# Copying turned attention probabilities out of PSUM with one engine or with two, one head each

## The reference

```python
# first block, per head
s_own = jnp.einsum('bhqd,bhpd->bhqp', qb, kown).astype(f32) * scale + bias_own
p = jax.nn.softmax(logits, axis=-1)
out = jnp.einsum('bhqp,bhpd->bhqd', p_own, vown)

# second block, per head
p_cmp = _softmax_f32(logits, valid) * valid
o_sel = jnp.einsum("bghtk,bgtkd->bghtd", p_sel, vs)
o_win = jnp.einsum("bghtk,bgkd->bghtd", p_win, vw)
out = gc[..., 0:1] * o_cmp + gc[..., 1:2] * o_sel + gc[..., 2:3] * o_win
```

## Time and profile before

| | us |
|---|---|
| median of 3 runs | 1717.1 (1715.51 to 1721.55) |
| the profiled execution's own time | 1719.34 |
| its span, first to last instruction | 1717.4 |
| TensorE busy in the span | 1679.1 |
| VectorE busy | 938.7 |
| ScalarE busy | 720.3 |

### The profile page before, as it was taken

How to read it: one execution, slowest core, us unless ns; L and a number is a source line. 1 busy time by engine, 2 the same in 40 slices (tenths; PEclk the granted TensorE clock), 3 DMA queues, 4 the chain that set the end, 5 groups by cost and what they waited for, 6 DMA issues and landing times.

```text
span 1717.4 us, 26172 instructions
## 1 busy us (share of the span) xinstructions
PE 1679.1 (98%) x11461; PEld 1530.6 (89%) x11466; DVE 938.7 (55%) x928; ACT 720.3 (42%) x822; POOL 58.9 (3%) x72
## 2 busy tenths in 40 slices
PE   8998999999999999999999999999999999899999
PEld 6987899989889998999989899998999987689998
DVE  5476644455564445554576545455545485754544
ACT  5404443444444344443443434345434334753432
POOL 0023000000000000000000000000000030000000
PEclk9999999999999999999999999999999998999999
DMA  9544546457354644655565564656564534036461
GB/s 294 186 75 124 190 163 216 155 184 231 123 190 167 216 154 171 221 183 185 176 208 167 174 209 157 212 172 201 191 220 150 194 117 160 2 130 213 152 217 74
DMA packets 221649, 297.15 MB, mean 173 GB/s; under 512 B 7403, under 2 KB 184767, under 8 KB 221536
## 3 DMA queue, kind: packets, MB, share of 16 engines
q1 hardware_dynamic: 215256, 284.39, 49.5%
q10 hardware_dynamic: 6280, 11.09, 2.8%
HBM read 291.27 MB, written 3.15 MB: 171 GB/s over the span
## 4 chain that ended last, share of the span: by engine, by line
PE 89%; DVE 5%; ACT 3%; DMA 2%; issue 1%; POOL 0%; SPq 0%; ACTq 0%; DVEq 0%; POOLq 0%
PE ps L1739 20%; PE ps L1639 16%; PE ps L1640 16%; PE ps L1642 16%; PE ps L1661 3%; PE ps L1655 3%; PE ps L1656 3%; DVE wlo L1087 2%; PE ps L1686 2%; PE ps L1687 1%; PE ps L1688 1%; ACT whi L623 1%; DMA raw<-in_hgrn_w_out 1%; PE ps L1677 1%; PE ps L2048 1%
## 5 line engine op out<-in xcount | busy, mean ns | idle before, releaser
L1087 DVE TENSOR_TENSOR wlo<-raw,whi 128x2048 fp32r<-128x2048 f32 (+2 forms) x270 | 602.5, 2251 | 228.7 <-ACT whi L623 228.1
L1639 PE MATMUL ps<-xhi,whi 128*128 128x256 f32 x2432 | 599.6, 284 | 4.8 <-DVE xlo L1113 4.8
L1640 PE MATMUL ps<-xhi,wlo 128*128 128x256 f32 x2432 | 597.7, 283 | 0.0
L623 ACT ACTIVATE whi<-raw 128x2048 fp32r<-128x2048 f32 (+1 forms) x265 | 497.9, 1900 | 114.4 <-DMA raw<-in_hgrn_w_out 40.3
L1639 PEld LDWEIGHTS ps<-xhi,whi 128*128 128x128 f32 x2432 | 467.2, 192 | 7.5 <-issue 5.2
L1640 PEld LDWEIGHTS ps<-xhi,wlo 128*128 128x128 f32 x2432 | 467.6, 192 | 2.3
L1642 PE MATMUL ps<-xlo,whi 128*128 128x256 f32 x2432 | 341.4, 283 | 0.0
L1642 PEld LDWEIGHTS ps<-xlo,whi 128*128 128x128 f32 x2432 | 313.7, 192 | 0.0
L690 ACT ACTIVATE hhi<-hid 128x512 fp32r<-128x512 f32 x54 | 34.1, 632 | 511.0 <-DVE hid L1150 461.1
L1150 DVE TENSOR_TENSOR hid<-silu,ps 128x512 f32<-128x512 f32 x60 | 41.3, 688 | 319.5 <-PE ps L1642 319.5
L1739 PE MATMUL ps<-whi,hhi 128*128 128x512 f32 x480 | 187.5, 391 | 0.0
(11 more groups left out here) (229 smaller groups left out, 1328.4 us busy)
## 6 DMA issues: line engine op xcount, KB each, us to landing
raw<-in_ffn_w_gate_up SPq DMA_DIRECT2D x80, 1024.0 KB, 5.6
raw<-in_ffn_w SPq DMA_DIRECT2D x62, 1024.0 KB, 5.7
raw<-in_ffn_w_down SPq DMA_DIRECT2D x44, 1024.0 KB, 5.6
raw<-in_hgrn_w_in SPq DMA_DIRECT2D x16, 1024.0 KB, 5.7
raw<-in_moba_w_in SPq DMA_DIRECT2D x12, 1024.0 KB, 5.7
raw<-in_conv_w_in SPq DMA_DIRECT2D x10, 1024.0 KB, 5.2
raw<-in_ffn_w_gate_up SPq DMA_DIRECT2D x16, 512.0 KB, 5.3
raw<-in_kv_w SPq DMA_DIRECT2D x6, 1024.0 KB, 5.1
```

Of the source, the lines that this page charges most:

```text
L623: act.activation(whi[s % WRING][:, 0:width], raw[n % RING][:, 0:width], ACT.Copy).then_inc(split_hi, 1)
L1087: ins = dve.tensor_tensor(wlo[s % WRING][:, part], raw[n % RING][:, part], whi[s % WRING][:, part].bitcast(F32), ALU.subtract)
L1639: pe.matmul(out, hi[:, k, tile], xhi[:, k, :], start=k == 0, stop=False)
L1640: pe.matmul(out, lo[:, k, tile], xhi[:, k, :], start=False, stop=False)
```

## The change

The copy of a unit's turned probabilities is divided by head. ScalarE copies the first head's 384 elements from bank 4 and signals `pt_ready` as before. VectorE copies the second head's 384 elements from bank 5 in a new function, `keep_other`, with a new semaphore, `pt_other_ready`. TensorE waits for both where it waited for one. In `attention`, `keep_other(i - 1)` is put on VectorE's queue directly behind `scale_probs(i - 1)`, ahead of `y_low` and of the maxima of the next iteration. In `moba` the copies stand at the head of the next unit's work. The new copy waits for the same two things as ScalarE's: the turn of this unit, and the values of two units before.

```diff
--- before.py
+++ after.py
@@ -381,6 +381,7 @@
         probs_ready = sem("probs_ready")
         probs_turned = sem("probs_turned")
         pt_ready = sem("pt_ready")
+        pt_other_ready = sem("pt_other_ready")
         pv_done = sem("pv_done")
         gate_kept = sem("gate_kept")
         gated = sem("gated")
@@ -821,7 +822,7 @@
                 act.wait_ge(probs_turned, at.att + u + 1)
                 if u >= 2:
                     act.wait_ge(pv_done, at.att + u - 1)
-                act.activation(att_pt[:, u % 2, :, :], ps[:, 4:6, 0:3 * P], ACT.Copy).then_inc(pt_ready, 1)
+                act.activation(att_pt[:, u % 2, 0, :], ps[:, 4, 0:3 * P], ACT.Copy).then_inc(pt_ready, 1)
 
             def y_high(pair, units, dst, src):
 
@@ -1334,6 +1335,13 @@
                         ins = dve.tensor_scalar(x, x, coef[:, b, n:n + 1], None, ALU.mult)
                 ins.then_inc(probs_ready, 1)
 
+            def keep_other(u):
+
+                dve.wait_ge(probs_turned, at.att + u + 1)
+                if u >= 2:
+                    dve.wait_ge(pv_done, at.att + u - 1)
+                dve.tensor_copy(att_pt[:, u % 2, 1, :], ps[:, 5, 0:3 * P]).then_inc(pt_other_ready, 1)
+
             def y_low(pair, dst, high, src):
                 dve.wait_ge(yhi_ready, at.y + pair + 1)
                 dve.tensor_tensor(dst, src, high.bitcast(F32), ALU.subtract).then_inc(ylo_ready, 1)
@@ -1346,6 +1354,7 @@
                         maxima(i, scale, 2 * (i % 2))
                     if 0 <= i - 1 < units:
                         scale_probs(i - 1, gate(i - 1))
+                        keep_other(i - 1)
                     if i >= 2 and (i - 1) % branches == 0:
                         pair = (i - 2) // branches
                         dst, src = pair_out(pair)
@@ -1375,6 +1384,8 @@
                 split(name, "q", 2)
                 dve.wait_ge(bias_landed, 32)
                 for u in range(3):
+                    if u >= 1:
+                        keep_other(u - 1)
                     if u == 1:
                         moba_low(0)
                     moba_max(u)
@@ -1388,10 +1399,12 @@
                     elif u < 2:
                         split(name, "out", 0)
                 moba_low(1)
+                keep_other(2)
                 moba_max(3)
                 split(name, "out", 2)
                 scale_probs(3)
                 moba_low(2)
+                keep_other(3)
                 split(name, "out", 3)
                 moba_low(3)
                 at.att += 4
@@ -1884,6 +1897,7 @@
                 pe.wait_ge(probs_ready, at.att + u + 1)
                 if u >= 1:
                     pe.wait_ge(pt_ready, at.att + u)
+                    pe.wait_ge(pt_other_ready, at.att + u)
                 for a in range(2):
                     for n in range(3):
                         mm = pe.transpose(ps[:, 4 + a, n * P:(n + 1) * P], att_l[:, u % 2, a, n * P:(n + 1) * P], ident)
@@ -1892,6 +1906,7 @@
             def values(u, pv, pair, first):
 
                 pe.wait_ge(pt_ready, at.att + u + 1)
+                pe.wait_ge(pt_other_ready, at.att + u + 1)
                 if pair and first:
                     pe.wait_ge(ylo_ready, at.y + pair)
                 pv(u, att_pt[:, u % 2]).then_inc(pv_done, 1)
```

## The result

The changed kernel takes 1734.35 us, the median of 5 executions (1731.58 to 1736.81), beside 1718.64 us for the kernel before (5 executions, 1715.51 to 1723.57). The ratio is 1.0087, with a 95% interval of 1.0070 to 1.0104: 15.7 us or 0.9% slower. The profiled execution took 1731.58 us with a span of 1729.8.

A forecast was written before the change was run, and what follows sets the result against it. A ring through TensorE, VectorE and ScalarE was taken to bound the sixteen units (6.57 us per two), within a mostly TensorE-bound program; +12.7 us for the loop less 0.3 at the tail, +12.4 on 1717.1, gave 1729.5, range 1725 to 1735.

The forecast's parts named there:

- rival 3: Second attention's sixteen units: VectorE waits for each turn before the next maxima; 1727 to 1733 us, chance 0.8.
- rival 4: Second attention: the same waiting plus TensorE's clock falling to half; between 1733 and 1761 us, chance 0.1.
- The loop: Second attention's sixteen units: turns 4.00 or 4.34 us apart, 61.25 us over 15 steps against 48.57.
- The durations: Second attention: VectorE's copy 0.55 us, 0.48 of its queue; ScalarE's copy 0.49; start of turn to copy 0.91.
- The first block: Copies in `moba`, among long projections, taken to cost nothing; bounds -0.3 to +0.6 us.
- The waits on TensorE: Second semaphore wait in front of each turn: taken as 0 us, upper end 0.9 us.
- The clock: Second attention's sixteen units: granted clock expected to hold at 1.00 despite idle gaps of 1.2 and 1.0 us.
- signs of being wrong: Sixteen units: maxima start before the turn ends, copy under 0.42 or over 0.7 us, or granted clock below 1.00.
- last step: Fifteenth to sixteenth turn of the second attention, with no maxima left: 3.21 us.
- Rival 1: Second attention: VectorE's copies fit by load and the wait is not paid; 3 us faster, 1714, chance 0.03.
- rival 2: Second attention: only the copy before `y_low` counts, the other hides; 1719 to 1721 us, chance 0.07.
- Short idle stretches: TensorE in the sixteen units: skill's rule of a swinging clock, not borne out before for gaps of 0.9 us.

The follow-up runs named there:

- experiment 1: Kernel before plus an empty VectorE wait, behind each scaling, until those probabilities are turned; no copy: 1725.10 us, ratio 1.0042, turns 54.33 us.
- experiment 2: Kernel before plus a VectorE product of 384 constants in the copy's place, behind no wait: 1719.12 us, ratio 1.0004, turns 48.88 us.
- late_copy: Changed kernel with VectorE's copy one iteration later, behind the next maxima: 1720.13 us, ratio 1.0007, turns 50.22 us.
- first_only: Copies shared in the first block's attention alone, the second's as in the kernel before: 1719.20 us, ratio 0.9999.
- after_warm: Changed kernel plus two matmuls of zeros before each turn from the second on; run twice: 1735.78 and 1735.21 us, ratios 1.0091 and 1.0093.
- both_late: Changed kernel with VectorE's copy and y's low part both behind the next maxima: 1718.49 us, ratio 0.9994, turns 46.56 us.
- y_late: Kernel before, ScalarE copying both heads, with y's low part one iteration later on VectorE: 1716.36 us, ratio 0.9983, turns 46.12 us.
- load_only: Kernel before plus a VectorE product of constants as long as the copy, behind no wait: 1719.12 us, ratio 1.0004.
- wait_only: Kernel before plus one VectorE wait for the turn behind each scaling, copying nothing: 1725.10 us, ratio 1.0042.
- y_first: Changed kernel with y's low part ahead of VectorE's copy: 1733.64 us, ratio 1.0079, turns 59.79 us.

## Why the prediction was right, and where it was short

Forecast were 1729.5 us in a range from 1725 to 1735, slower with a chance of 0.9; measured were 1734.35. The forecast was 12.4 us on a median before of 1717.1; that median is 1718.64 over five executions, and the measured difference 15.7. The direction and the mechanism were right. But 1734.35 lies above the 1727 to 1733 of the closed loop (rival 3) and inside the range only by its margin for the spread of medians and for the mild end of rival 4, so that the range held is in part luck. By its steps:

- **The loop** held to 0.03 us a step: 3.98 for 4.00 and 4.31 for 4.34. Over the first fourteen steps that is 57.68 us in the trace for 58.04. The wait alone (experiment 1: 5.76 us) and the copy alone (experiment 2: 0.3 us) show that the wait closes the loop and that the copy costs only inside it, and `late_copy` that it is the place on the queue.
- **The durations** held: 0.56 for 0.55, 0.47 for 0.48 to the next start, 0.49 for 0.49 on ScalarE, 0.92 for 0.91 from the turn to the copy (1460.70 to 1461.62).
- **The first block** at nothing held (`first_only`, 0.9999), the thin cover of 0.04 us before the third unit's maxima included.
- **The waits on TensorE** at nothing held: the scaling at 1463.62 is followed by the turn at 1464.68, 1.06 us later, where it was 1.07.
- **The clock** is the term that was mis-sized. The forecast took it at nothing, because TensorE is busy for 2.80 of 4.00 us in the loop with single gaps of 1.2. That is so while there are scores. The last two units have none, and I had not worked out how long TensorE idles in them: the turn at 1506.12 has 1.49 us of idle time before it and the compressed values 1.07, and from 1504 to 1508 TensorE is busy for 1.51 of 4.00 us. Behind these the clock falls, at 1508.1, ahead of the sixteenth turn, so one of the forecast's own signs of being wrong came: a granted clock below 1.00 in this stretch. In the profiled execution the fall costs 1.1 us in the last step (4.47, where 3.34 was due at full clock), 1.4 up to the output product (3.77 for 2.4) and 1.8 in it, 4.3 us. Without it the last three of the four parts above (13.58, 1.19 and 1.80, together 16.6 us) would be 12.3, beside the 12.4 of the sum. In the medians, the 3.3 us beyond the forecast go with the lower mean clock of the table above; in which stage the executions other than the profiled ones pay them stays open. This is the mild end of rival 4, to which I gave a tenth of the chance; it came on top of rival 3 and not in its place. A single fall was counted there as 3.4 us of half clock and at most 1.7 us of time; it was 10.2 us of half clock.
- **The profiled span** of 1729.8 us, the forecast to a tenth, is chance: the 4.3 us that the fall costs were given back but for some 0.1 ahead of the stretch, where this execution had a higher clock than the profiled one of before.
- **In the last step** the forecast, 3.21 us, also missed a wait: the values of a pair's first branch need y's low part of the pair before, which is now behind the copy (1.07 us at 1508.07), and the last turn stands behind these values on TensorE's queue. In the trace of `after_warm`, at full clock, TensorE is done with the values 3.34 us after the start of the fifteenth turn (1514.47 to 1517.81), so the wait is worth 0.13 us.
- **Rival 1** (the copies fit by load, 3 us faster) and **rival 2** (half of the stall covered) are out: the maxima start 1.53 us later than the scaling allows (1462.09 for 1460.56), where 1.55 was counted.
- **Short idle stretches.** The clock is at 1.00 over 54 us with gaps of 0.9 and 1.1 us, and at half behind the gaps of 1.49 and 1.07. The Trainium skill, "TensorE: Matmul & The Clock Gate", section "A second HAM failure mode: psum-queue depth-cycling", says that frequent short idle stretches can make the gate swing. The trace agrees for the last units at most, and with one fall, not a swing.

## What to carry to other kernels

When work is moved to an engine with time to spare, ask where on its queue it stands and what it waits for, before asking how long it takes: a wait for the consumer of the instruction just issued closes a loop over both engines, and here 0.47 us of copy came with 0.97 us of idle time at each unit. Put such a copy behind the work that the next round needs (here one iteration later), and check by a wait without the work whether it is the wait or the work that costs. And with the loop open, what counted was TensorE's own work: `both_late` against `y_late` shows that the split of the copy did not pay there either (46.56 and 46.12 us for the stretch).

## What the runs showed of the hardware that I had not expected

Sums of starts and steps read from one trace carry over to other orders of the queues to a few hundredths of a microsecond a step, some tenths over the fifteen: the turns of `load_only` were 0.3 us longer where 0.5 at most were expected, those of `wait_only` 54.33 for 54.0, of `late_copy` 50.2 for 50, of `y_first` 59.8 for 60.3, of `y_late` 46.1 for 46.5, of `both_late` 46.6 for 47. What doesn't carry over is TensorE's clock: the same kernel's spans run from 1711 to 1722 us over 66 executions, in step with the mean granted clock (0.996 down to 0.989), so a trace says what a stage costs, and its total only together with its clock.
